# Twenty projection tiles moved out of one block, one by one between the steps of what follows

## The reference

```
u = rms_norm(x); proj = u @ w_in                      # D_MODEL 1024 -> 43 tiles of 128 columns
z, xbc, dt, xm, i, f, o, cq, ckv, kr, xq = split(proj)
A: conv + silu on xbc, SSD scan (chunks of 128), + d_skip, * silu(z_a), grouped rms_norm
B: conv + silu on xm, mLSTM scan (exp input gate, forget gate), sigmoid(o) * h, rms_norm, * silu(z_b)
C: q = norm(norm(cq) @ w_uq), k = norm(latent @ w_uk), rotary parts; softmax(q k) @ latent @ w_uv, * silu(z_c)
   (prompt: causal over itself; each request: over 2048 cached latents in 16 pages, and itself)
D: q = norm(xq), attention over 256 memory tokens, * silu(z_d)
x = x + concat(A, B, C, D) @ w_out
```

## Time and profile before

| what | value |
|---|---|
| median of 3 runs | 1514.53 us (1510.49 to 1523.02) |
| profiled execution | 1522.11 us, span 1520.4 us |
| PE busy | 1387.2 us (91%) |
| DVE, ACT busy | 602.8 us, 430.3 us |
| granted clock of PE, mean | 0.936 |
| first projection product of layer 1, layer 2 | 22.17 us, 767.97 us |

### The profile page before, as it was taken

The page is one execution under the profiler, slowest core; times in us unless marked ns, Lnnn a source line. Parts: engine busy times, 40 slices in busy tenths (PEclk is TensorE's granted clock), DMA queues, the critical chain, the costliest instruction groups (busy, mean ns, idle before and its releaser), DMA issues. The chain is left out here.

```text
span 1520.4 us, 23108 instructions
## 1 busy us (share of the span) xinstructions
PE 1387.2 (91%) x7072; PEld 1127.3 (74%) x7072; DVE 602.8 (40%) x1308; ACT 430.3 (28%) x1035; POOL 83.5 (5%) x144
## 2 busy tenths in 40 slices
PE   6999998888989899998979999988888999999797
PEld 5788864556878787876868887656577888878586
DVE  3000063553755555562120003454355555555611
ACT  1000343511434343440000005333123444434300
POOL 0000000000000000000000000000000000000000
PEclk9999998977999999999989999999589999999789
DMA  6634430021444444401474344201042444444022
GB/s 267 217 138 159 147 122 29 1 72 45 151 152 154 152 152 152 153 30 57 140 256 154 138 152 155 78 18 58 14 139 79 144 149 157 148 157 153 15 87 107
DMA packets 92485, 184.15 MB, mean 121 GB/s; under 512 B 15051, under 2 KB 66004, under 8 KB 80598
## 3 DMA queue, kind: packets, MB, share of 16 engines
q1 hardware_dynamic: 76838, 98.94, 19.9%
q0 software_dynamic: 10944, 75.76, 14.4%
q10 hardware_dynamic: 4608, 8.39, 1.5%
HBM read 169.15 MB, written 13.90 MB: 120 GB/s over the span
## 5 line engine op out<-in xcount | busy, mean ns | idle before, releaser
L513 PE MATMUL ps<-wk,scr 128*128 128x258 f32 x2048 | 472.7, 385 | 0.0
L513 PEld LDWEIGHTS ps<-wk,scr 128*128 128x128 f32 x2048 | 383.4, 192 | 51.0
L425 PE MATMUL ps<-uT,ring 128*128 128x264 f32 x1376 | 311.6, 390 | 15.2 <-DVE uT L1270 10.9
L425 PEld LDWEIGHTS ps<-uT,ring 128*128 128x128 f32 x1376 | 264.1, 192 | 62.8 <-issue 16.9
L1126 DVE TENSOR_REDUCE ssq<-scr 128x4 f32<-128x512 f32 x256 | 170.6, 681 | 153.7 <-ACT scr L909 152.5
L909 ACT ACTIVATE scr<-ps 128x512 f32<-128x512 f32 x256 | 151.5, 594 | 2.1 <-DVE ssq L1126 2.0
L830 PE MATMUL ps<-pt,ring 128*128 128x264 f32 x512 | 123.0, 401 | 3.9 <-DVEq L1521 3.9
L1284 DVE COPY pt<-ps 128x264 f32 x40 | 17.3, 433 | 269.6 <-PE ps L425 269.6
L830 PEld LDWEIGHTS ps<-pt,ring 128*128 128x128 f32 x512 | 100.6, 198 | 22.7 <-issue 4.9
L906 ACT ACTIVATE raws<-ps 128x4 f32<-128x4 f32 x256 | 44.2, 173 | 236.1 <-PE ps L513 235.9
L500 PE MATMUL ps<-cst,lat 128*128 128x128 f32 x512 | 82.7, 285 | 16.9 <-DMA lat<-in_lat 12.6
(11 more groups left out here) (294 smaller groups left out, 1372.4 us busy)
## 6 DMA issues: line engine op xcount, KB each, us to landing
ring<-in_weights POOLq DMA_DIRECT2D x68, 1024.0 KB, 5.1
lat<-in_lat SPq DMA_DIRECT2D x256, 128.0 KB, 2.9
rows<-rowscr SPq DMA_DIRECT2D x16, 1024.0 KB, 7.2
kr<-in_krope SPq DMA_DIRECT2D x256, 32.0 KB, 2.0
uT<-in_memv SPq DMA_DIRECT2D x16, 512.0 KB, 3.6
uT<-in_memk SPq DMA_DIRECT2D x16, 512.0 KB, 5.5
states<-in_ssm SPq DMA_DIRECT2D x16, 256.0 KB, 3.5
states<-in_mlC SPq DMA_DIRECT2D x16, 256.0 KB, 5.0
```

Of the source, the lines that this page charges most:

```text
L425: last = mm(ps[:, bank, 0:T], w[:, k, :], u3[:, k, :], start=k == 0, stop=k == KT - 1)
L513: last = mm(ps[:, 1 + 2 * (j % 2) + half, 0:258], latT[:, g % 2, q, c, :], wk[:, 2 * c + half, at:at + 258], start=c == 0, stop=c == 1)
```

## The change

The first 23 tiles stay in one block. The other 20 run later: tile 23 right behind the block, 34 to 41 between the steps of the norm chain, 42 and 24 around the first scores, 25 to 27 in attention heads 1, 3 and 5, and 28 to 33 behind recurrence steps 1, 3, 5, 7, 8 and 9. All 20 share PSUM bank 7, one at a time. The convolution and the gates are written among the copies of tiles 12 to 21, so under the first block. What had to make room:

- PSUM banks of the norm chain, the scores (three banks and not four), the masked products (one bank and not two).
- The weights of the memory keys and values and of the queries no longer pass through the ring. SP loads them into `lat0` (`big`). The first request's latents, which lay there from the layer's start, are loaded in two halves: after the query products, and after the last recurrence step (`ry_mm` 12). The recurrences' `dec` lies in the upper half of `lat0` too.
- Latent pages have two signals, lower and upper 8 pages; PE waits for the upper ones only at the fourth pair (`g == 3`).
- SiLU is split: convolution and z of groups C and D before the first exp of the attention, z of A and B and the output gate's sigmoid after the recurrences.
- At the start x is loaded and summed before the memory tokens. The root of x's squares moves from behind `layer_free` to before it.

```diff
+LOOPED = 20
+FIRST_TILES = 23
+LATER_TILES = (23, *range(34, 43), *range(24, 34))
+TILE_ORDER = (*range(FIRST_TILES), *LATER_TILES)
+FILL_BANK = 7
+RING_IN = (*range(12), *range(17, 22), 12, 13, 28, 29, 14, 15, 16)
+FILL_HEADS = {1: 25, 3: 26, 5: 27}
+FILL_STEPS = {1: 28, 3: 29, 5: 30, 7: 31, 8: 32, 9: 33}
-S_BANK = (7, 6, 0, 1)
+S_BANK = (0, 1, 6)
+        big = [A0[:, 0:SLOT], A0[:, SLOT:2 * SLOT]]
+        dec = A0[:, SLOT:SLOT + 1536].rearrange("p (u i) -> p u i", u=4)
...
 @block.sync
+                load_big(l, R_MK, 0)
+                load_big(l, R_MK, 1)
-                load_latents(0, places)
...
+                sp.wait_ge(*n_in(l, 3))
+                load_latents(0, places, 0, PAGES // 2)
...
+                high = places_of(l, 0)
+                sp.wait_ge(*ry_mm(l, 12))
+                load_latents(0, high, PAGES // 2, PAGES)
...
 @block.tensor
+            def later(l, m):
+
+                i = LATER_TILES.index(m)
+                at = RING_IN.index(m // 2)
+                slot(l, at)
+                pe.wait_ge(*fill_out(l, i))
+                tile_mm(l, m, at % 2, m % 2, FILL_BANK)
...
             def masked(l, item):
-                if item >= 2:
-                    pe.wait_ge(*st_out(l, item - 1))
+                if item:
+                    pe.wait_ge(*st_out(l, item))
...
             def sample(l, b, u, before, pages_now, pages_next):
                 for g in range(8):
+                    if g == 3:
+                        pe.wait_ge(*lat_high[u](l, 16 * 8 * pages_now))
...
+                product(4)
+                later(l, 35)
+                pe.wait_ge(*n_out(l, 3))
+                product_sums(3)
+                later(l, 36)
+                product_sums(4)
+                product(5)
+                later(l, 37)
...
+                scores(l, 0)
+                for h in range(HEADS + 1):
+                    last = mm(ps[0:ROPE, 2 + h, 0:T], cst[0:ROPE, K_ROT:K_ROT + ROPE], QR[:, h, :], start=True, stop=True)
+                last.then_inc(r_mm.sem, 1)
+                later(l, 42)
+                scores(l, 1)
+                later(l, 24)
                 pe.wait_ge(*r_out(l, 1))
+                scores(l, 2)
...
 @block.scalar
+                act.wait_ge(*conv_d(l, 1))
+                act.wait_ge(*fill_out(l, LATER_TILES.index(42) + 1))
+                fn(xc[:, :, :], xc[:, :, :], ACT.Silu).then_inc(xc_ready.sem, 1)
+                fn(pt[:, Z + 8:Z + 16, :], pt[:, Z + 8:Z + 16, :], ACT.Silu).then_inc(z_ready.sem, 1)
+                nc.scalar.preload_act_table_set(LN_EXP)
                 probs(l, 0)
+                later_out(24)
...
+                    if n - 2 in FILL_STEPS:
+                        later_out(FILL_STEPS[n - 2])
+                act.drain()
+                fn(pt[:, Z:Z + 8, :], pt[:, Z:Z + 8, :], ACT.Silu)
+                fn(pt[:, OG:OG + 4, :], pt[:, OG:OG + 4, :], ACT.Sigmoid).then_inc(z_ready.sem, 1)
...
+                act.wait_ge(*x_ss(l, 1))
+                root(nrs[:, 0, :], ps[:, 4, 0:T], 1.0 / D_MODEL).then_inc(x_rs.sem, 1)
                 act.drain().then_inc(layer_free.sem, 1)
...
 @block.vector
+                tile_out(15)
                 dve.wait_ge(*conv_a(l, 1))
+                dve.wait_ge(*pj_act(l, CT // 2))
                 tap(2)
+                tile_out(17)
...
                 for k in range(3, 9):
+                    later_out(k + 32)
                     dve.wait_ge(*n_rs(l, k + 1))
...
                 tt(QR[:, :, :], QR[:, :, :], t, ALU.add).then_inc(r_out.sem, 1)
+                later_out(42)
```

More of the change, by code:

```diff
@@ L271, in load_rotary, with load_latents, load_big @@
                     half = ROPE * (j // 8)
[L272 to L276, removed]
+                    sp.dma_start(kr[half:half + ROPE, u, j % 8, :], one("krope", page)).then_inc(lat_low[u].sem, 16)
+            def load_latents(u, places, first=0, end=PAGES):
+                for j in range(first, end):
+                    done = lat_low[u] if j < PAGES // 2 else lat_high[u]
+                    sp.dma_start(latb[u][:, j, :], one("lat", places[j])).then_inc(done.sem, 16)
+            def load_big(l, n, c, wide=SLOT):
+                weights = d["weights"][bass.ds(CHUNKS * l + (n + c), 1)].rearrange("o p n -> p (o n)")
+                sp.dma_start(big[c][:, 0:wide], weights[:, 0:wide]).then_inc(big_in[c].sem, 16)
             def load_values(l, b):
@@ L611, in _ @@
                                       start=c == 0 and k == 0, stop=c == 1 and k == 3)
[L612 to L618 removed]
+                    last.then_inc(big_used.sem, 1)
+                sums(l, 2, 0, [[(P, nsq[0][:, 2 * i:2 * i + 2, 0:MEM])] for i in range(2)], 2 * MEM)
@@ L674, in _ @@
-                pe.wait_ge(*n_out(l, 9))
+                    sums(l, k, N_SUMS, [[(n, nsq[k % 2][0:n, h, :])] for h in range(2)])
+                pe.wait_ge(*n_out(l, 1))
+                pe.wait_ge(*n_rs(l, 3))
+                big_slot(l, 2, 0)
+                product(3)
+                pe.wait_ge(*mv_out(l, 1))
+                big_slot(l, 2, 1)
+                product(4)
[3 more added lines that the diff above has]
+                later(l, 36)
@@ L675, in _ @@
+                product_sums(4)
+                product(5)
+                later(l, 37)
+                product_sums(5)
+                product(6)
+                later(l, 38)
+                product_sums(6)
+                pe.wait_ge(*wsm_in(l, 32))
+                product(7)
+                later(l, 39)
+                product_sums(7)
+                product(8)
+                later(l, 40)
+                product_sums(8)
+                pe.wait_ge(*n_out(l, 8))
                 for m in range(2):
-                    if m:
-                        for h in range(HEADS + 1):
-                            last = mm(ps[0:ROPE, h, 0:T], cst[0:ROPE, K_ROT:K_ROT + ROPE], QR[:, h, :], start=True, stop=True)
-                        last.then_inc(r_mm.sem, 1)
@@ L684, in _ @@
+                scores(l, 0)
[5 more added lines that the diff above has]
+                later(l, 24)
                 pe.wait_ge(*r_out(l, 1))
-                pe.wait_ge(*lv_out(l, 1))
-                for h in range(3):
-                    scores(l, h)
+                scores(l, 2)
```

405 lines of the change are left out of this document (216 added, 189 removed).

## The result

Over four runs each on one chip the changed kernel took 1465.0 us in the median (1461.9 to 1465.7) and the kernel before 1515.8. The ratio is **0.966, 95% interval [0.962, 0.970]**. The forecast was 1454 with a range of 1434 to 1482: faster, as said, and inside the range, but 11 us too hopeful. Run twice more, the same kernel gave 0.963 [0.960, 0.966] and 0.965 [0.962, 0.968]. Two executions of the experiments ran in a slower state (1615.2 us of the second control, 1453.4 us of the kernel with all three edits) and are left out of their kernels' medians. The profiled execution took 1465.7 us, 56.4 less than the one profiled before.

A forecast was written before the change was run, and what follows sets the result against it. PE bounds the kernel; only its idle or low-clock time can be won. 2 x (8.4 + 0.7 + 17.6) + 12.6 + 1.5 - 1.2 - 2.0 = 64.3 off 1522.1 gave 1457.8, taken as 1454 us, range 1434 to 1482.

The forecast's parts named there:

- Stretch one: Tile 8 to the first transposes: idle 9.8 and low clock 8.5 us fall to 9.9 in all, saving 8.4 a layer.
- the one wait foretold: Ahead of attention's first transposes: ACT waits for tile 42's copy before the first exp, so PE waits 5.9 us a layer.
- Recurrences: Six tiles among the recurrence steps: 62.2 us against 79.8, saving 17.6 a layer, bounds about 3 to 21.
- Steps 0 and 1 and half of tile 28: Start of the recurrences: the part still at low clock, 3.4 us of lengthening a layer.
- the wait of 1.8 at step 7: Recurrences, the only odd gap without a tile before it: 1.8 us, counted within 7.1 us of idle time.
- The 18.6 us that I called low clock: Recurrences before the change: PE busy 46.9 us against 28.3 of work at full clock, the difference taken as low clock.
- Rival 1: Clock returns only in part, falling again between tiles: recurrences save 8, stretch one 6; 24 us less, 1478; chance 0.17.
- Requests: PE's four waits for latents, 12.6 us in both layers, go through the split into halves: saving 12.6 for both.
- Start and border: Loading x first saves 1.5 us at the start; the root before `layer_free` costs 1.2 at the layers' border.
- Rival 2: More comes back: wait before the first exp costs little, clock holds; up to 20 us more, 1436; chance 0.14.
- Rivals 3, 4 and 5: 3: waits return elsewhere, 1495, chance 0.06; 4: low clock through filled stretches, up to 1597, 0.03; 5: no gain, 1514, 0.03.
- the middle between two readings of the first run's 7.6 us: Profiled execution's excess over the median: returning low clock gives 1457.8, a shift of all 1450.2; forecast took 1454.

The follow-up runs named there:

- second control: The changed kernel run again without edits, as base of the two kernels run with it: 1462.4 us, 0.965 of the kernel before.
- all three edits: Changed kernel with tile 28 ahead of step 0, tile 31 behind step 6, convolution's SiLU before the wait for tile 42's copy: 1436.7 us, 0.946.
- the first of the kernels above: Changed kernel with tile 31 behind recurrence step 6 and not step 7: 1454.5 us, 0.958 of the kernel before.
- the controls: The changed kernel run twice more without edits, as measure for its variants: 1462.1 us (0.963) and 1462.4 us (0.965).

## Why the prediction was right, and where not

**What bounds the kernel: right.** PE's idle time and its low clock were what the change could win, and both fell, 33 and 23 us in the profiled pair.

**Stretch one: right in mechanism, one us a layer too small** (18.9 us saved in both layers behind tile 16, 16.8 said). The chain's waits are gone but for 0.38 us, and the one wait foretold stands at its place, 3.48 us and not 5.9. I had put the table load of 1.28 us on the path, and ACT does it while it waits: SiLU starts the moment the copy of tile 42 is done, and the load stands 10 us ahead of that.

```profile
203.61 1.28 ACT L1099 ACT_TABLE_LOAD   x1
214.30 2.85 ACT L1099 ACTIVATE xc<-xc 128x3168 f32<-128x3168 f32 x1 [9.40 <-DVE pt L1390]
...
219.01 1.28 ACT L1101 ACT_TABLE_LOAD   x1
```

From DVE's rotation (209.36) to the transposes (222.49) it is 13.1 us against 14.8 said, and PE had 9.7 us of its own and not 8.9. With SiLU first, 2.7 of the 3.5 us went: the order of ACT's queue made the wait. TensorE: Matmul & The Clock Gate, a page of the Trainium skill, has ScalarE strictly in queue order under "Architectural detail"; that trace agrees.

**Recurrences: the step that failed.** "Steps 0 and 1 and half of tile 28", 3.4 us of lengthening a layer, was this term's low clock, and it measured 8.6, by rows at either level. First fall: masked product 0.8, steps 0 and 1 with their spreads 2.5, tile 28 1.9 (5.73 less 3.83), together 5.2. Second fall, not foreseen: masked product 0.8, spread 1.0, tile 31 1.6, together 3.4. The idle time was as forecast (69.08 - 62.27 = 6.8 us against 7.1), with the waits where they were said, 2.70 and 1.70. Busy time was 62.27 us for 49.7 of work; 12.6 less 8.6 leaves 4.0 for handovers, where I had chosen 2.0. So 17.6 - 5.2 - 2.0 = 10.4, and 10.7 was measured. One mistake was to price the wait of 1.8 at step 7 at 1.8: the row of the kernel before with a step's wait of 1.70, stands in a stage at 0.68, and told that such waits go with a low clock. Where an edit undid the first or the second fall, both layers together gave 12.6 and 7.6 us, their waits included.

A second mistake lay in what there was to win. The 18.6 us that I called low clock were all of PE's busy time beyond its work at full clock. In the windows 319.50:336.60, 340.00:343.40 and 346.80:363.90 of the kernel before, all at 0.50, PE is busy for 32.3 us; at half clock that is a loss of 16.1, and the other 2.5 were handovers already. The same count for the changed kernel (284.30:297.90 and 318.40:325.20, busy 17.7 us) gives 8.9. So the clock gave back 7.2 us a layer where the forecast had 15.2, while the waits gave 4.7 against 4.4.

**Rival 1 was half right.** The clock did fall again between one tile and the next, once, and moving one tile into the gap ahead of step 7 took that fall away. What decides a fall is not shown. At the end of the gap left open it came behind waits of 1.30 to 1.70 us in most traces, and in the first of the kernels above 1.30 us were passed without one. At the start of the stage it came ahead of the 2.70 us wait, the nearest wait before it being 0.99. Under "HAM oscillation — how this bites in real kernels" the same page of the Trainium skill lays low clock to long waits between bursts; by that the stretch would have held the full clock, and this trace does not agree.

**Requests: right in mechanism, too small by 4.3 us.** The latents' waits went from 12.6 to 0.7 us (2.3 and 3.4 in the controls). By the windows of both stages PE's idle time fell by 9.1 us, not by all of the 11.9, since other waits grew; the other 7.8 us are busy time. Of these, 3 are the half clock behind the wait of 3.54. Behind the other three waits there was none, so the rest, half clock at other places, is not shown to come from the waits; this stage also differs by up to 4 us, both layers together, among the three executions of the changed kernel.

**Start and border: right.** 2.0 us against 1.5; the wait at the border grew by 0.5 and not 1.2 (7.80 to 8.31).

**Rival 2 came true in one part,** the smaller wait before the first exp; the clock did not hold. **Rivals 3, 4 and 5 fell:** no wait of the chain came back, and tiles 29 and 30 stand at 3.83 us.

**One term was missing, and its sign changes from run to run.** The output projection's first 16 us can run at either clock. Kernel before, then after; windows of 16 us from the stage's first product, layer 1:

```profile
696.32:712.00 15.68, 15.68 (x82) 13.76 (x83) 2.77 (x13) 0.00 (x0) 0.74 (x1) 1.00 0.19 68
```

```profile
663.84:680.00 16.16, 16.16 (x48) 13.58 (x49) 1.91 (x11) 0.00 (x0) 0.00 (x0) 0.50 0.01 1
680.00:684.00 4.00, 4.00 (x19) 3.35 (x19) 0.86 (x2) 0.00 (x0) 0.74 (x1) 0.97 0.11 16
```

In layer 2 it was the reverse: 1439.80 to 1456.00 at 0.50 before, and 1389.80 to 1406.00 at 0.89 after. No tile was moved to or from this stretch, and each that is wholly low costs 8 us. In the profiled pair the two nearly cancel (-2.1 us). In the two controls only 0 to 7 us of it a layer were low. My choice of the middle between two readings of the first run's 7.6 us was a guess; that this stretch made the 7.6 us is not shown.

**Left open:** what decides the output's clock. Behind a softmax wait of 6.0 to 6.1 us and one of 1.7 to 2.3 it ran its first 16 us low in one layer and all or mostly at full clock in the other, in both kernels. It was low within 1 us too when the long wait was filled (the one right ahead of it then being 4.0 us). No kernel here removed both.

## What to carry to other kernels

Price a short wait of TensorE by its length plus the slow products that may stand behind it, as a chance and not as a rule: here a wait of 1.7 us among short products cost 3.4 more in layer 1, and one for latents of 3.5 about 3 more, but the kernel before had three more waits of 2.6 to 3.4 us that cost nothing beyond their length. Fillers pay where they stand *between* dependent steps (the same six in a block ahead of them were 13 to 18 us a layer worse), and the first belongs ahead of the first step, where the longest wait is. And when an in-order engine gets a new wait in front of its queue, move what doesn't need it ahead: moving one line took away 5.4 us of waits and gave 9.8 in the medians, and with the filler's move the kernel came to 1436.8 us, 0.948 of the first.

## What the runs showed of the hardware

- The clock can stay at 0.50 while PE is busy all the time with full 128 x 128 products: 16.16 of 16.16 us in the output projection. In tile 28 of the changed kernel it came back: 5.73 us for the tile against 3.83 at full clock.
- Products with operands 8 and 64 wide can run on at the full clock once it is there: busy 5.02 of 5.30 us at 1.00 in one layer and 5.08 of 5.35 in the other, with tile 28 ahead of step 0. With all six tiles in a block ahead of them, they fell to half clock after 2 us in layer 1.
- The same wait of 1.30 us at step 8 was followed by a fall in one kernel and by none in another; of four waits for latents of 2.6 to 3.5 us in the kernel before, one was.
- The clock fell at the start of the recurrences (284.3 in the changed kernel, 994.4 with tile 28 ahead of step 0) where the nearest wait before it was 0.99 us.
